# Masked products, updates and sampled updates of a linear attention, split into parts with a mixer product between the parts

## The chip, the cores and the metric

The kernel runs on one core of a Trainium2 chip. The metric is the device time of one launch in microseconds (us). Three runs of the kernel before gave 2438.61, 2433.31 and 2435.87 us; their median, 2435.87 us, is the time before. Engines are named as the profile names them: PE is TensorE with its matmuls, PEld its weight loads, DVE is VectorE, ACT is ScalarE, POOL is GpSimd, SP the engine that issues most loads.

## The reference

The reference is one step of a hybrid decoder of two layers (DEPTH = 2) over a prompt of 512 tokens and a sample group of 8 sequences with 4 new tokens each, 544 token rows in all. Each layer has two token mixers in parallel, a sparse attention (its output is A) and a gated linear attention, GLA (its output is B), and then a gated merge and a feed-forward part:

```python
def step(S, inp):
    qi, ki, vi, gi = inp
    b = jnp.cumsum(gi, axis=2)
    qe = qi * jnp.exp(b)
    att = jnp.where(tril, jnp.einsum('bhid,bhjd->bhij', qe, ki * jnp.exp(-b)), 0.0)
    o = jnp.einsum('bhij,bhjv->bhiv', att, vi) + jnp.einsum('bhid,bhdv->bhiv', qe, S)
    bl = b[:, :, -1:, :]
    S = jnp.exp(bl[:, :, 0, :, None]) * S + jnp.einsum('bhjd,bhjv->bhdv', ki * jnp.exp(bl - b), vi)
    return S, o
...
mix = jax.nn.sigmoid(g_ma) * (o_a @ w_pa) + jax.nn.sigmoid(g_mb) * (o_b @ w_pb)
x = x + mix @ w_out
```

GLA has 4 heads with keys of 64 and values of 128. The prompt's 512 tokens are 8 chunks of 64, in which the state S is carried from chunk to chunk; each of the 8 sampled sequences has one chunk of 4 tokens and a state of its own. The change touches `att` (the masked product), the last einsum of `step` (the update of the state) for the prompt and for the sampled sequences, and the order in which they stand to `o_a @ w_pa`. Everything is fp32.

## The kernel before

Every engine has a program of its own, written out by hand in the order in which it is to run; PE's begins at L788 and runs the two layers in a loop, and ACT and DVE have loops of the same shape. They are held together by semaphores alone. The activations stand transposed, features on the partitions and the 544 tokens in the free dimension, so that a product of a 128-column block of a weight is a chain of matmuls over the 128-row blocks of the contraction, each in two halves of 272 tokens (`product`, L809). In the trace each such matmul shows as two instructions with a weight load each.

PSUM has pools of slots that are taken in turn: T and S with two slots each, of two banks, and E. `claim` waits until the use of the slot before this one has been drained, that is until ACT or DVE has copied it out; `filled` is what the draining engine waits for. A product named X therefore cannot start on PE before the product two places ahead of it in the same pool has been drained. The names are tickets: `pa0` to `pa7` (the mixer products, T), `att0` to `att4` (the masked products, S), `up0` to `up7` (the updates of the prompt's state, T), `us0` to `us3` (the updates of the sampled states, T, two sequences each), `kd` and `kd4` (transposes of the decayed keys, S), `o8s`, `o8` (outputs of the sampled sequences, S), `o0` to `o3` (outputs of the four prompt tiles, S), and `on0` to `on3` (the sums of squares for the output norm, T).

The part in question comes once per layer, between the end of the sparse attention's softmax work and the merge:

- PE transposes the decayed keys (`kd`, L1264, and `kd4`, L1269), and ACT copies both out (L1708 to L1713).
- `first_mixer(m)` (L1275) is one of the eight 128-column blocks of `o_a @ w_pa`: four blocks of contraction, two halves, 16 matmuls in the trace with 128x272 outputs. It needs AT, whose last part DVE writes (`at_ready`). DVE's `gate_mixer(m)` (L2341) multiplies it out of PSUM with the merge gate, which ACT's sigmoid over `gaT` has to have made (`merge_gate`).
- The masked products (L1284 to L1294): for each of the four prompt tiles of 128 tokens, the 4 heads' products of 64x128 keys and 64x128 queries, and a small fifth for the sampled tokens. DVE multiplies each with a mask as it copies it out.
- The updates (L1298 to L1308): 8 chunks, 4 heads each, 64x64 weights. DVE adds each to the state carried on (`stt` at L2379, each needs the one before).
- `o8s` and `o8`: what the sampled queries read from their old states, and their outputs. Then the sampled updates (L1335 to L1343), which DVE adds to S0 after it has scaled S0 (L2391).
- `o0` to `o3` (L1345 to L1357): the prompt's outputs from masked products, values and states. ACT copies each out (L1726 to L1729).
- `out_norm(h)` (L1359): `mean_d` times the squares of head h. ACT squares all four heads after it has copied `o3` out (L1733, 1734), then takes the roots (`norm_root`, L424), and DVE turns each into the normed and gated output.

PE's order before is: `kd`, `kd4`, mixers 0 and 1, masked 0 to 4, mixer 2, updates 0 to 7, mixer 3, `o8s`, mixer 4, `o8`, sampled updates 0 to 3, mixer 5, `o0` to `o3`, mixer 6, `on0`, `on1`, mixer 7, and then the gate products `gb` and the products `pb` of the second mixer.

DVE's order before is: the last copies into AT, memsets and copies that spread the queries over `qz` and `qzs` (L2350 to L2361), `gate_mixer(0)`, the five masks, gates 1 and 2, the eight steps of the state, `kdb`, gates 3 and 4, the scaling of S0, the four sampled additions, gates 5 and 6, then the norms.

POOL writes the new states out after `gla_states` 1 and 2 and brings x back to its tile after `o3`; SP loads the mixer weights `pa0` and `pa1` into ring slots well ahead and refills each slot when its last product is filled.

Of the kernel before, what the change touches and what calls it, by code (L numbers as in the profile page):

```python
# [26 lines left out]
ALU = mybir.AluOpType  # L27
# [3 lines left out]
P = 128  # L31
D_MODEL, SEQ, DEPTH, NB, TS = 1024, 512, 2, 8, 4
PAST, PAGE = 2048, 128
HD, HEADS, G, R = 64, 8, 2, 4
STRIDE = 16
NS = NB * TS
# [11 lines left out]
GH, DK, DV, RANK = 4, 64, 128, 16  # L48
GL_HALF, GL_ROWS = 64, 104
CHUNK = 64  # L50
# [180 lines left out]
def build(nc, S, ins, outs):  # L231
# [3 lines left out]
    with ctx:  # L235
# [5 lines left out]
        PS = ctx.enter_context(nc.psum_tensor("PS", [P, 8, 512], F32))  # L241
# [22 lines left out]
        gmask_s = sb("gmask_s", NS)  # L264
# [77 lines left out]
        vT = xrows[:, 0:2560].rearrange("p (t n) -> p t n", n=512)  # L342
# [444 lines left out]
        def _(pe):  # L787
# [90 lines left out]
            for l in range(DEPTH):  # L878
# [396 lines left out]
                def first_mixer(m):  # L1275

                    w = ring[:, wload(f"pa{m // 4}"), :].rearrange("p (r n) -> p r n", n=512)
                    c0 = P * (m % 4)
                    product("T", f"pa{m}", lambda k: w[:, k, c0:c0 + P], lambda k: AT[:, k, :], R)

                pe.wait_ge(*S.at(pe, "at_ready", 1))
                first_mixer(0)
                first_mixer(1)
                for t in range(5):  # L1284

                    pe.wait_ge(*S.claim(pe, "S", f"att{t}"))
                    b = S.banks(pe, f"att{t}")
                    pe.nop().then_inc(*S.inc(pe, "settled"))
                    n = P if t < 4 else NS
                    for h in range(GH):  # L1290
                        hp, o = h // 2, HD * (h % 2)
                        mm = pe.matmul(PS[0:n, b + h % 2, n * hp:n * hp + n], kbT[o:o + HD, hp, P * t:P * t + n], qbT[o:o + HD, hp, P * t:P * t + n],
                                       start=True, stop=True)
                    mm.then_inc(*S.fill(pe, f"att{t}"))  # L1294
                first_mixer(2)


                for t in range(4):  # L1298
                    for c in range(2):
                        i = 2 * t + c  # L1300
                        pe.wait_ge(*S.claim(pe, "T", f"up{i}"))
                        b = S.banks(pe, f"up{i}")
                        pe.nop().then_inc(*S.inc(pe, "settled"))
                        for h in range(GH):
                            o = HD * (h % 2)
                            mm = pe.matmul(PS[o:o + HD, b, P * (h // 2):P * (h // 2) + P], kdm[CHUNK * c:CHUNK * c + CHUNK, t, HD * h:HD * h + HD],
                                           vT[CHUNK * c:CHUNK * c + CHUNK, t, P * h:P * h + P], start=True, stop=True)
                        mm.then_inc(*S.fill(pe, f"up{i}"))  # L1308
                first_mixer(3)
                pe.wait_ge(*S.at(pe, "qke_ready", 1))  # L1310
                pe.wait_ge(*S.at(pe, "s0_in"))
# [20 lines left out]
                        out = PS[:, b, 0:GH * NS].rearrange("p (a c f n) -> p a f c n", a=2, c=2, f=2)[:, a, hf]  # L1332
                        mm = pe.matmul(out.rearrange("p c (q t) -> p c q t", t=TS), o8s[:, hf, a, :], of_row, start=False, stop=(a == 1 and hf == 1))
                mm.then_inc(*S.fill(pe, "o8"))
                for q in range(4):  # L1335
                    pe.wait_ge(*S.claim(pe, "T", f"us{q}"))
                    b = S.banks(pe, f"us{q}")
                    for i in range(2):
                        for h in range(GH):
                            o = HD * (h % 2)  # L1340
                            mm = pe.matmul(PS[o:o + HD, b, 256 * i + P * (h // 2):256 * i + P * (h // 2) + P], kdb[0:NS, 2 * q + i, HD * h:HD * h + HD],
                                           vT[0:NS, 4, P * h:P * h + P], start=True, stop=True)
                    mm.then_inc(*S.fill(pe, f"us{q}"))  # L1343
                first_mixer(5)
                pe.wait_ge(*S.drained(pe, "att3"))  # L1345
                for t in range(4):
                    pe.wait_ge(*S.at(pe, "state", 1))
# [7 lines left out]
                            mm = pe.matmul(PS[:, b, P * h + CHUNK * c:P * h + CHUNK * c + CHUNK], states[:, i, h // 2, :],  # L1355
                                           qz[:, h, CHUNK * i:CHUNK * i + CHUNK], start=False, stop=(c == 1))
                    mm.then_inc(*S.fill(pe, f"o{t}"))  # L1357
                first_mixer(6)
                def out_norm(h):  # L1359

                    pe.wait_ge(*S.at(pe, "sq_o", h + 1))
# [435 lines left out]
        def _(dv):  # L1797
            S.phase(dv, "pro")

            def tt(out, a, b_, op):  # L1800
                return nc.vector.tensor_tensor(out, a, b_, op)  # L1801
# [16 lines left out]
            def bc(v, shape):  # L1818
                return v.broadcast_to(shape)
# [42 lines left out]
            for l in range(DEPTH):  # L1862
# [478 lines left out]
                def gate_mixer(m):  # L2341

                    dv.wait_ge(*S.filled(dv, f"pa{m}"))
                    b = S.banks(dv, f"pa{m}")
                    dv.wait_ge(*S.at(dv, "merge_gate", 1))
                    tt(two(gaT[:, m, :]), pair2(b), two(gaT[:, m, :]), ALU.mult).then_inc(*S.drain(dv, f"pa{m}"))
# [13 lines left out]
                    last = copy(qzs[:, :, :, TS * c:TS * c + TS],  # L2360
                                qz[:, c:GH:2, SEQ:NT].rearrange("p a (b t) -> p b a t", t=TS))  # L2361
                last.then_inc(*S.inc(dv, "qke_ready"))
                gate_mixer(0)
                for t in range(4):
                    dv.wait_ge(*S.filled(dv, f"att{t}"))
                    b = S.banks(dv, f"att{t}")
                    tt(attT[:, t].rearrange("p (a o) n -> p o a n", o=2), PS[:, b:b + 2, 0:256].rearrange("p o (a n) -> p o a n", a=2),
                       bc(gmask[:, :].unsqueeze(1).unsqueeze(1), [P, 2, 2, P]), ALU.mult).then_inc(*S.drain(dv, f"att{t}"))
                dv.wait_ge(*S.filled(dv, "att4"))
                b = S.banks(dv, "att4")  # L2370
                tt(att_s[0:NS].rearrange("p (a o) n -> p o a n", o=2), PS[0:NS, b:b + 2, 0:2 * NS].rearrange("p o (a n) -> p o a n", a=2),
                   bc(gmask_s[0:NS, :].unsqueeze(1).unsqueeze(1), [NS, 2, 2, NS]), ALU.mult).then_inc(*S.drain(dv, "att4"))
                gate_mixer(1)
                gate_mixer(2)
                for i in range(8):
                    dv.wait_ge(*S.filled(dv, f"up{i}"))
                    b = S.banks(dv, f"up{i}")
                    for c in range(2):
                        last = stt(states[:, i + 1, c, :], states[:, i, c, :], eb[:, c, CHUNK * i + CHUNK - 1:CHUNK * i + CHUNK],  # L2379
                                   PS[:, b, P * c:P * c + P], ALU.mult, ALU.add)  # L2380
                    last.then_inc(*S.drain(dv, f"up{i}"))
                    dv.wait_ge(*S.drained(dv, f"up{i}"))
                dv.nop().then_inc(*S.inc(dv, "gla_states"))
                dv.wait_ge(*S.drained(dv, "kd4"))
                tt(kdb[0:NS, :, :], bc(kdm[0:NS, 4, :].unsqueeze(1), [NS, NB, 256]), bc(batch_hot[0:NS, :].unsqueeze(2), [NS, NB, 256]), ALU.mult).then_inc(*S.inc(dv, "kdb"))
# [5 lines left out]
                    last = tt(S0[:, :, a, :], S0[:, :, a, :], bc(ebS[:, :, a:a + 1], [P, NB, DV]), ALU.mult)  # L2391
                last.then_inc(*S.inc(dv, "dve_step"))
                dv.wait_ge(*S.last(dv, "dve_step"))
                for q in range(4):
                    dv.wait_ge(*S.filled(dv, f"us{q}"))
                    b = S.banks(dv, f"us{q}")
                    v = S0[:, 2 * q:2 * q + 2, :, :].rearrange("p b a v -> p (b a v)")
                    tt(v, PS[:, b, :], v, ALU.add).then_inc(*S.drain(dv, f"us{q}"))
                dv.wait_ge(*S.drained(dv, "us2"))
                dv.wait_ge(*S.drained(dv, "us3"))  # L2400
                dv.nop().then_inc(*S.inc(dv, "gla_states"))
                gate_mixer(5)
                gate_mixer(6)
                for h in range(GH):
                    if h == 1:
# [108 lines left out]
```

## Time and profile before

| | |
|---|---|
| median of three runs | 2435.87 us (2433.31 to 2438.61) |
| the profiled execution | 2436.56 us, its span 2434.8 us |
| PE busy | 2385.6 us, 98% of the span |
| DVE, ACT busy | 809.5 us (33%), 539.0 us (22%) |
| mean granted TensorE clock | 0.986 |
| the stretch from `kd4` to the end of mixer 7, first layer | 515.0 to 580.8 us of the span |
| the same in the second layer | 1719.4 to 1785.2 us |

How to read it: the span is the time from the first to the last instruction of one profiled execution, and positions such as 515.0 are microseconds from its start. Busy shares say how full an engine is; the granted clock is the share of full speed that TensorE was given, 1.00 for 2.4 GHz and 0.50 for 1.2 GHz. In the answers below each line of the timeline has a start, a length, the engine, the line of the kernel, the operation, what it writes and reads, its shape and how many instructions were merged into it; in square brackets stands the idle time before them and what ended it.

### The profile page before, as it was taken

What the parts mean: (1) busy time and instruction counts of PE and PEld (TensorE: products, weight loads), DVE (VectorE), ACT (ScalarE), POOL (GpSimd) and SP (SyncE); (2) the same over time, 40 slices, a digit from 0 to 9 for tenths busy, and PEclk for the clock granted to TensorE, in tenths of its full rate; (3) what the DMA queues carried; (4) which work ended last, traced back from release to release, by engine and by line L of the source; (5) the groups of instructions that cost most, each with busy time, mean ns of one, the idle gap of its engine ahead of it and who ended that gap; (6) DMA issues with size and microseconds to landing.
All of it is one profiled execution on the core that took longest, in us unless ns stands there. A gap on an engine that the chain in (4) does not pass through costs nothing.

```text
span 2434.8 us, 30974 instructions
## 1 busy us (share of the span) xinstructions
PE 2385.6 (98%) x13063; PEld 1926.0 (79%) x13063; DVE 809.5 (33%) x1893; ACT 539.0 (22%) x1085; POOL 104.8 (4%) x190
## 2 busy tenths in 40 slices
PE   8999899999999999999999999999999999999999
PEld 7787766678888888888888877667788888888887
DVE  4554545544114222210035544465441232222000
ACT  2353124432011111110013522244220111111000
POOL 4010010001000000000000100000000000000000
PEclk9999999999999999999999999999899999999999
DMA  7553421112222222212373544111122222222222
GB/s 231 186 200 142 197 95 52 32 41 89 70 72 70 70 78 79 66 51 72 77 265 130 219 162 183 53 36 36 49 95 72 69 70 70 70 82 65 63 72 73
DMA packets 186988, 237.55 MB, mean 98 GB/s; under 512 B 38047, under 2 KB 172704, under 8 KB 181984
## 3 DMA queue, kind: packets, MB, share of 16 engines
q1 hardware_dynamic: 175208, 133.11, 18.4%
q0 software_dynamic: 11200, 102.36, 11.1%
q8 instruction: 104, 1.70, 0.3%
q14 instruction: 32, 0.26, 0.0%
q10 hardware_dynamic: 444, 0.12, 0.0%
HBM read 222.76 MB, written 21.11 MB: 100 GB/s over the span
## 4 chain that ended last, share of the span: by engine, by line
PE 93%; DVE 4%; DMA 1%; ACT 1%; issue 1%; SPq 0%; POOL 0%; DVEq 0%; ACTq 0%; POOLq 0%
PE PS L818 52%; PE PS L1441 13%; PE PS L840 6%; PE PS L938 4%; PE PS L866 2%; DVE arena L1810 2%; PE PS L926 2%; PE PS L437 2%; PE PS L1219 2%; PE PS L1208 2%; PE PS L1136 1%; DMA arena<-in_cache_kv_slc_dram,idx 1%; ACT arena L1472 1%; PE PS L1181 1%; PE PS L1147 1%
## 5 line engine op out<-in xcount | busy, mean ns | idle before, releaser
L818 PE MATMUL PS<-hT,ring 128*128 128x272 f32 x4352 | 1010.1, 394 | 2.5 <-DVE small L2254 1.9
L818 PEld LDWEIGHTS PS<-hT,ring 128*128 128x128 f32 x4352 | 827.9, 191 | 175.5 <-issue 8.7
L1472 ACT ACTIVATE arena<-PS 64x512 f32<-64x512 f32 (+13 forms) x467 | 231.3, 518 | 1185.8 <-PE PS L818 559.8
L1441 PE MATMUL PS<-arena,ring 128*128 128x272 f32 x1408 | 323.7, 393 | 0.0
L1441 PEld LDWEIGHTS PS<-arena,ring 128*128 128x128 f32 x1408 | 268.0, 191 | 54.1
L1810 DVE COPY arena<-PS 64x512 f32<-64x512 f32 (+4 forms) x201 | 142.7, 710 | 268.6 <-PE PS L818 98.4
L1801 DVE TENSOR_TENSOR arena<-PS,arena 128x544 f32<-128x544 f32 (+3 forms) x124 | 76.0, 624 | 398.2 <-PE PS L818 380.9
L818 PE MATMUL PS<-arena,ring 128*128 128x272 f32 x768 | 177.2, 393 | 3.1 <-DVE arena L1801 3.1
L818 PEld LDWEIGHTS PS<-arena,ring 128*128 128x128 f32 x768 | 146.2, 191 | 33.5 <-DVE arena L1801 4.0
L1807 DVE SCALAR_TENSOR_TENSOR arena<-arena,prm 128x32 f32<-128x32 f32 (+1 forms) x176 | 88.1, 500 | 249.1 <-ACT arena L1472 245.8
L1801 DVE TENSOR_TENSOR xT<-PS,xT 128x544 f32<-128x544 f32 x32 | 23.2, 724 | 386.3 <-PE PS L1441 303.2
L840 PE MATMUL PS<-ring,hT 128*128 128x256 f32 x640 | 146.3, 390 | 0.6 <-ACT qT L1472 0.6
L840 PEld LDWEIGHTS PS<-ring,hT 128*128 128x128 f32 x640 | 124.1, 196 | 21.8 <-issue 3.3
L938 PE MATMUL PS<-arena 128*128 128x256 f32 (+1 forms) x576 | 136.5, 382 | 2.3 <-DVE arena L1810 0.5
L938 PEld LDWEIGHTS PS<-arena 128*128 128x128 f32 x576 | 103.2, 198 | 19.5 <-DVE arena L1810 5.2
L1472 ACT ACTIVATE arena<-arena 128x544 f32<-128x544 f32 (+5 forms) x102 | 68.1, 694 | 73.1 <-DVE arena L1807 71.5
L1472 ACT ACTIVATE arena<-xT,prm 128x544 f32<-128x544 f32 x32 | 23.5, 745 | 266.4 <-DVE xT L1801 264.7
L1472 ACT ACTIVATE arena<-arena,small 128x128 f32<-128x128 f32 (+3 forms) x128 | 70.4, 556 | 40.4 <-DVE small L1807 39.9
L926 PE MATMUL PS<-ident,arena 128*128 128x128 f32 (+1 forms) x576 | 73.0, 270 | 0.0
L818 PE MATMUL PS<-qT,ring 128*128 128x272 f32 x256 | 70.2, 435 | 0.0
L926 PEld LDWEIGHTS PS<-ident,arena 128*128 128x128 f32 (+1 forms) x576 | 63.6, 142 | 7.6 <-issue 1.5
L818 PEld LDWEIGHTS PS<-qT,ring 128*128 128x128 f32 x256 | 53.2, 213 | 13.9 <-issue 2.1
(309 smaller groups left out, 1665.3 us busy)
## 6 DMA issues: line engine op xcount, KB each, us to landing
ring<-in_w_up_dram SPq DMA_DIRECT2D x88, 512.0 KB, 4.6
ring<-in_w_in_dram SPq DMA_DIRECT2D x68, 512.0 KB, 4.8
ring<-in_w_down_dram SPq DMA_DIRECT2D x32, 384.0 KB, 3.8
ring<-in_w_down_dram SPq DMA_DIRECT2D x32, 320.0 KB, 4.5
arena<-in_state_kv_win_dram POOLq DMA_DIRECT2D x4, 2048.0 KB, 20.4
ring<-in_w_out_dram SPq DMA_DIRECT2D x16, 512.0 KB, 4.1
out_dram<-in_state_kv_win_dram POOLq DMA_DIRECT2D x2, 4064.0 KB, 23.8
ring<-in_w_in_dram SPq DMA_DIRECT2D x16, 256.0 KB, 5.0
```

Source lines behind the costliest of these rows:

```text
L437: mm = pe.matmul(PS[HD * g:HD * g + HD, VBANKS[qt % 2], P * r:P * r + P], kv[:, t, 1 + br, P + HD * g:P + HD * g + HD], PTp[j % 2][:, g, P ...
L818: mm = pe.matmul(PS[0:m, b + a, 0:HALF], weight(k), rhs(k)[:, HALF * a:HALF * a + HALF], start=(k == 0), stop=(k == nk - 1))
L840: mm = pe.matmul(out, hT[:, k, P * t:P * t + nt], w[:, k, c0:c0 + n], start=(k == 0), stop=(k == KC - 1))
L866: mm = pe.matmul(PS[:, b + a, 0:HALF], w[:, k, P * i:P * i + P], raw[:, k, HALF * a:HALF * a + HALF], start=(k == 0), stop=(k == KC - 1))
L926: mm = pe.transpose(PS[:, b + r // 4, P * (r % 4):P * (r % 4) + n], XB[s][0:n, 8 * q + r, P * c:P * c + P], ident[0:n, 0:n])
L938: mm = pe.matmul(out, w1[:, c, 4 * q + pr, :, :], XT[j % 2][:, pr, :, 0:n], start=(q == 0 and pr == 0), stop=(q == 1 and pr == 3))
L1208: mm = pe.matmul(PS[:, b + g, 0:P * (qt + 1)], qT[HD * g:HD * g + HD, r, P * qt:P * qt + P], kT[HD * g:HD * g + HD, br, 0:P * (qt + 1)], s ...
L1441: mm = pe.matmul(PS[:, b + a, 0:HALF], w[:, k, :], aT[:, 11 * half + k, HALF * a:HALF * a + HALF], start=(half == 0 and k == 0), stop=(hal ...
L1472: return nc.scalar.activation(out, in_, func, **kw)
L1801: return nc.vector.tensor_tensor(out, a, b_, op)
L1807: return nc.vector.scalar_tensor_tensor(out=out, in0=a, scalar=s_, in1=b_, op0=op0, op1=op1)
L1810: return nc.vector.tensor_copy(out, a)
```

## The change

Nothing is computed differently. On PE the masked and the update products become helpers, and the order is: masked 0 to 2, mixer 0, masked 3 and 4, mixer 1, updates 0 to 3, mixer 2, updates 4 to 7, mixer 3, `o8s`, mixer 4, `o8`, sampled updates 0 and 1, mixer 5, sampled updates 2 and 3, mixer 6, `o0` to `o3`, `on0`, `on1`, mixer 7. On DVE the masks, the steps of the state and the additions move in the same manner against the gates: three masks come ahead of gate 0. ACT, POOL and SP are as before. (The diff is cut to its moved calls; the bodies of the helpers are those shown above.)

```diff
 # PE
-                pe.wait_ge(*S.at(pe, "at_ready", 1))
-                first_mixer(0)
-                first_mixer(1)
-                for t in range(5):
+                def masked(t):
...
+                def update(i):
...
+                for t in range(3):
+                    masked(t)
+                pe.wait_ge(*S.at(pe, "at_ready", 1))
+                first_mixer(0)
+                for t in range(3, 5):
+                    masked(t)
+                first_mixer(1)
+                for i in range(4):
+                    update(i)
                 first_mixer(2)
-                for t in range(4):
-                    for c in range(2):
-                        i = 2 * t + c
...
+                for i in range(4, 8):
+                    update(i)
                 first_mixer(3)
...
-                for q in range(4):
+                def sampled_update(q):
...
+                sampled_update(0)
+                sampled_update(1)
                 first_mixer(5)
+                sampled_update(2)
+                sampled_update(3)
+                first_mixer(6)
                 pe.wait_ge(*S.drained(pe, "att3"))
                 for t in range(4):
...
                     mm.then_inc(*S.fill(pe, f"o{t}"))
-                first_mixer(6)
 # DVE
-                gate_mixer(0)
-                for t in range(4):
+                def masked(t):
...
-                gate_mixer(1)
-                gate_mixer(2)
-                for i in range(8):
+                def update(i):
...
+                for t in range(3):
+                    masked(t)
+                gate_mixer(0)
+                masked(3)
+                dv.wait_ge(*S.filled(dv, "att4"))
...
+                gate_mixer(1)
+                for i in range(4):
+                    update(i)
+                gate_mixer(2)
+                for i in range(4, 8):
+                    update(i)
...
-                for q in range(4):
+                def sampled_update(q):
...
+                sampled_update(0)
+                sampled_update(1)
+                gate_mixer(5)
+                sampled_update(2)
+                sampled_update(3)
                 dv.wait_ge(*S.drained(dv, "us2"))
                 dv.wait_ge(*S.drained(dv, "us3"))
                 dv.nop().then_inc(*S.inc(dv, "gla_states"))
-                gate_mixer(5)
                 gate_mixer(6)
```

## Rows read from the trace of the kernel before

**Rows 1.** The page, part 1 (busy time) and part 4 (chain that ended last, by engine)

```profile
PE 2385.6 (98%) x13063; PEld 1926.0 (79%) x13063; DVE 809.5 (33%) x1893; ACT 539.0 (22%) x1085; POOL 104.8 (4%) x190
...
PE 93%; DVE 4%; DMA 1%; ACT 1%; issue 1%; SPq 0%; POOL 0%; DVEq 0%; ACTq 0%; POOLq 0%
```

**Rows 2.** Table by stretch, first layer; after the busy times: clock, DMA share, GB/s

```profile
515.00:530.00 15.00, 14.28 (x93) 11.46 (x94) 8.67 (x19) 8.91 (x6) 0.00 (x0) 1.00 0.11 37
530.00:536.40 6.40, 5.32 (x65) 3.64 (x62) 4.79 (x15) 0.00 (x0) 0.00 (x0) 0.89 0.01 3
536.40:543.00 6.60, 6.60 (x22) 4.85 (x24) 2.88 (x3) 0.00 (x0) 0.74 (x1) 0.59 0.08 22
...
549.80:555.10 5.30, 5.30 (x65) 4.74 (x65) 3.15 (x4) 0.28 (x1) 0.00 (x0) 0.71 0.01 3
555.10:560.80 5.70, 5.70 (x19) 4.47 (x18) 0.69 (x1) 0.00 (x0) 4.22 (x6) 0.67 0.32 98
```

**Rows 3.** Timeline, first layer, from `kd4` to DVE's first gate

```profile
514.19 1.30 ACT L1472 ACTIVATE arena<-PS 128x1024 f32<-128x1024 f32 x2 [9.89 <-PE PS L1264]
...
515.01 7.57 PE L818 MATMUL PS<-qT,ring 128*128 128x272 f32 x32
...
519.64 0.30 DVE L1810 COPY arena<-arena 128x64 f32<-128x64 f32 x2
...
520.74 0.72 DVE L1801 TENSOR_TENSOR arena<-PS,arena 128x544 f32<-128x544 f32 x1 [0.81 <-ACT arena L1472]
```

**Rows 4.** Timeline, first layer, masked products, mixer 2, updates, start of mixer 3

```profile
522.51 1.16 PE L1292 MATMUL PS<-qbT,kbT 64*128 64x128 f32 x16
523.27 1.29 DVE L1801 TENSOR_TENSOR kv_kT<-PS,gmask 128x512 f32<-128x512 f32 x2 [1.80 <-PE PS L1292]
...
524.11 1.31 PE L1292 MATMUL PS<-qbT,kbT 64*128 64x128 f32 x16 [0.44 <-DVE kv_kT L1801]
...
525.95 3.94 PE L818 MATMUL PS<-qT,ring 128*128 128x272 f32 x16
...
529.81 0.66 PE L1306 MATMUL PS<-xT,arena 64*64 64x128 f32 x8
...
532.30 1.29 PE L1306 MATMUL PS<-xT,arena 64*64 64x128 f32 x16 [0.34 <-DVE kv_kT L1807]
...
536.37 6.59 PE L818 MATMUL PS<-qT,ring 128*128 128x272 f32 x16
```

**Rows 5.** Timeline, first layer, from `o8`'s first matmul to mixer 5

```profile
547.77 1.07 PE L1327 MATMUL PS<-arena,xT 32*128 32x32 f32 x8
...
549.78 1.72 PEld L1341 LDWEIGHTS PS<-xT,arena 32*64 32x64 f32 x32
...
550.99 1.50 DVE L1801 TENSOR_TENSOR arena<-PS,arena 128x512 f32<-128x512 f32 x2
...
555.10 5.78 PE L818 MATMUL PS<-qT,ring 128*128 128x272 f32 x16
```

**Rows 6.** Timeline, first layer, from the end of `o3` to mixer 7

```profile
571.38 3.89 PE L818 MATMUL PS<-qT,ring 128*128 128x272 f32 x16
...
572.25 2.30 ACT L1472 ACTIVATE arena<-arena 128x544 f32<-128x544 f32 x4
574.57 1.28 ACT L1472 ACT_TABLE_LOAD   x1
...
575.10 2.23 PE L818 MATMUL PS<-arena,mean_d 128*128 128x272 f32 x8
...
576.22 0.71 ACT L1472 ACTIVATE kbT<-PS,cols 128x544 f32<-128x544 f32 x1 [0.37 <-PE PS L818]
...
577.16 3.83 PE L818 MATMUL PS<-qT,ring 128*128 128x272 f32 x16
```

**Rows 7.** Timeline, second layer: mixer 3, sampled updates, mixer 5

```profile
1740.65 5.22 PE L818 MATMUL PS<-qT,ring 128*128 128x272 f32 x16
...
1752.68 6.33 PE L1341 MATMUL PS<-xT,arena 32*64 32x128 f32 x64
...
1758.94 6.30 PE L818 MATMUL PS<-qT,ring 128*128 128x272 f32 x16
```

More of the change, by code:

```diff
@@ L1294, in _ @@
                     mm.then_inc(*S.fill(pe, f"att{t}"))
-                first_mixer(2)
-                for t in range(4):
-                    for c in range(2):
-                        i = 2 * t + c
[L1301 to L1308, printed above, removed]
+                def update(i):
+                    t, c = i // 2, i % 2
+                    pe.wait_ge(*S.claim(pe, "T", f"up{i}"))
+                    b = S.banks(pe, f"up{i}")
+                    pe.nop().then_inc(*S.inc(pe, "settled"))
+                    for h in range(GH):
+                        o = HD * (h % 2)
+                        mm = pe.matmul(PS[o:o + HD, b, P * (h // 2):P * (h // 2) + P], kdm[CHUNK * c:CHUNK * c + CHUNK, t, HD * h:HD * h + HD],
+                                       vT[CHUNK * c:CHUNK * c + CHUNK, t, P * h:P * h + P], start=True, stop=True)
+                    mm.then_inc(*S.fill(pe, f"up{i}"))
+                for t in range(3):
[7 more added lines that the diff above has]
+                    update(i)
+                first_mixer(2)
+                for i in range(4, 8):
+                    update(i)
                 first_mixer(3)
@@ L2368, in _ @@
                        bc(gmask[:, :].unsqueeze(1).unsqueeze(1), [P, 2, 2, P]), ALU.mult).then_inc(*S.drain(dv, f"att{t}"))
[L2369 to L2372, printed above, removed]
-                gate_mixer(1)
-                gate_mixer(2)
-                for i in range(8):
+                def update(i):
                     dv.wait_ge(*S.filled(dv, f"up{i}"))
@@ L2382, in _ @@
                     dv.wait_ge(*S.drained(dv, f"up{i}"))
+                for t in range(3):
[3 more added lines that the diff above has]
+                dv.wait_ge(*S.filled(dv, "att4"))
+                b = S.banks(dv, "att4")
+                tt(att_s[0:NS].rearrange("p (a o) n -> p o a n", o=2), PS[0:NS, b:b + 2, 0:2 * NS].rearrange("p o (a n) -> p o a n", a=2),
+                   bc(gmask_s[0:NS, :].unsqueeze(1).unsqueeze(1), [NS, 2, 2, NS]), ALU.mult).then_inc(*S.drain(dv, "att4"))
+                gate_mixer(1)
[4 more added lines that the diff above has]
+                    update(i)
                 dv.nop().then_inc(*S.inc(dv, "gla_states"))
```

## The prediction

> **What bounds the kernel now.** I read the page first: PE is busy for 98% of the span and carries 93% of the chain that ended last [rows 1]. So a change of order is worth what it does to PE's own line: its idle time, and its clock. Then the table by stretch for the part that the change touches, for the clock [rows 2], and then the timeline of the same part, for who waits for whom [rows 3 to 6]. The second layer repeats the first 1204.4 us later (mixer 0 at 1719.4 for 515.0) and differs only in where the clock falls [rows 7].
>
> In the table the clock is at full speed from 515.0 to 530.0, masked products included, and falls in two places [rows 2]. A mean of 0.89 over the 6.4 us of the updates is 1.4 us at half speed, so the clock fell near 535.0, some 5 us into them; then 5.4 us of the stretch with mixer 3 are at half speed (0.59 of 6.6 us). A mean of 0.71 in the sampled updates is 3.1 us at half speed, and 3.8 us more follow under mixer 5. What PE did before each fall was small products: the updates of 64x64 weights at the pace of DVE's additions, and `o8` and the sampled updates with 32 rows [rows 4, 5]. What it costs: mixer 3 takes 6.59 us where mixer 2 takes 3.94 (+2.65), mixer 5 takes 5.78 (+1.84), and the sampled updates last 5.32 us (549.78 to 555.10), where 32 of their 64 loads took 1.72 us at full speed, so some 3.6 in all (+1.7) [rows 4, 5]. That is 6.2 us. In the second layer it is 5.22 - 3.94 = 1.28, 6.30 - 3.94 = 2.36 and 6.26 - 3.6 = 2.7 [rows 7], 6.3 us. **12.5 us, 0.5% of the time, is all that the clock can give back here.**
>
> **The masked products, moved ahead of mixer 0.** Now mixers 0 and 1 run from 515.01 for 7.5 us, and under them DVE fills `qz`, until 519.94, and ACT makes the sigmoid that gate 0 waits for [rows 3]. The masked products come at 522.51, when DVE is nearly free. In the new order `att0` and `att1` can go as soon as ACT has drained `kd` and `kd4` (515.5), and are done by about 516.3. `att2` needs the slot of `att0`, which DVE drains, and DVE's first mask is still queued behind the `qz` copies: it starts at 519.95, takes 0.65 (half of 1.29), and from such a drain to PE's next start it is 0.15 (the first of the two masks from 523.27 ends at 523.95, `att2` starts at 524.11) [rows 4]. So `att2` starts at 520.75 and mixer 0, behind it, at 521.3. Queued behind that wait are `att2`, mixer 0 and all the rest of PE's line; mixer 0 itself would have needed nothing. Masked 3 and 4 later cost 0.7, half of the 1.16 of a pair and a small one of 0.2, with no wait left. Together 6.3 + 0.7 = 7.0 us, where the five took 3.44 (522.51 to 525.95): **+3.55 us** per layer. PE idles for 4.4 of these.
>
> **The updates in two groups.** Eight take 6.56 us (529.81 to 536.37) at DVE's pace. The first of a group finds its slot free; from the first's start to the fourth's it is 2.49 (532.30), plus 0.6 for the fourth itself (0.66 for eight instructions): 3.1 us for a group, 6.2 for two [rows 4]: **-0.35 us**. Gates 1 and 2 stand at the head of each group on DVE, as both do before the first now.
>
> **The sampled updates in two groups.** Mixer 5 takes the slot of `us0`, whose addition ends at 551.7, since DVE scales S0 until then [rows 5]; it can start 2.0 us after 549.78. Behind mixer 5, `us3` needs mixer 5's slot, which gate 5 (0.72) drains about 1.0 us after `us2` begins, so that group takes 2.0 too. 4.0 against 3.6 at full speed: **+0.4 us**.
>
> **Mixer 6, taken from behind `o3`.** It now runs from 571.38, while ACT copies `o3` out, squares four heads (until 574.55), loads the table for the roots (until 575.85) and takes the first root; `on0` and `on1` follow at 575.10, mixer 7 at 577.16 [rows 6]. So behind `o3` there are 577.16 - 571.38 = 5.78 us, 3.72 of them mixer 6. Without it `on0` waits for the first square (about 572.9), `on1` follows, and mixer 7 needs the slot of `on0`, which the root drains: 575.85 + 0.71 + 0.15 = 576.7. That is 5.35 us in place of 2.06: **+3.3 us**, with PE idle for 3.5 of them. ACT's work is what was hidden, and its cover is gone.
>
> At nothing I cost: DVE's gates and POOL's stores, which come a few us later but aren't waited for before the merge, 30 us on; SP's queue, where the load behind `pa0`'s slot waits for mixer 3 and that behind `pa1`'s for mixer 7, and each is wanted only after the gate products; and the reading of the squares on DVE, whose normed heads are wanted 30 us later.
>
> With the clock at full speed throughout, a layer is thus 3.55 - 0.35 + 0.4 + 3.3 = **6.9 us longer**, against 6.25 that the clock costs now.
>
> **What the clock costs after the change.** No row shows PE idle for 4.4 us in this part. From below it is nothing, if the clock stayed. I take it that it falls, since it fell under the updates, where PE still worked for 5.32 of 6.40 us [rows 2], and this stretch is emptier. What a fall costs the products behind it is in four rows: 1.28, 1.84, 2.36, 2.65 us, mean 2.0 [rows 4, 5, 7]. So mixer 0 and its neighbours lose 2.0. The stretch from `o8` to `us1` is 4.0 us of small products where now 7.3 stand (547.77 to 555.10); the clock fell 4.3 us into it (552.0), so an even chance of a loss of 2.6 (2.0, and some of the sampled updates themselves): 1.3. Each group of updates is 3.1 us where the clock fell after 5: one in four, 2.0 each, 1.0 for the two. Sum 4.3. **Per layer 6.9 - 6.25 + 4.3 = +4.95, for two +9.9 us.** The profiled execution took 2436.56, so 2446.5; it stands 0.7 above the median of the runs, so **2445.8 us**.
>
> The row shows the clock falling under a busy PE whose products are small. The Trainium skill ("TensorE: Matmul & The Clock Gate", section "HAM oscillation — how this bites in real kernels") says that bursts of matmuls with waits between them lose the clock again and again, and asks for denser work. Its advice speaks for the split of the updates and against the wait ahead of mixer 0; taken for the splits alone it is the first rival below.
>
> **Rivals.**
>
> *Faster: the clock decides.* If the splits hold the clock at full speed and the two waits turn out hidden, a layer gains 6.25 + 0.35 - 0.4 = 6.2: 2423.5 us. For it: each group of small products is shorter than what PE had done of them before the clock fell. It decides from the point where the two waits together cost less than 6.2 us of the 6.85 that I give them, with no new fall. Against it: the mask is behind 5 us of copies on DVE, ACT's chain behind `o3` is fixed, and PE has nothing to run in between. 0.08.
>
> *No difference.* The waits are as I say, but the clock stays up in the short idle stretch or costs the least seen, 1.28, and never falls elsewhere: +0.65 to +1.95 per layer, 2437 to 2440 us. 0.14.
>
> *Slower still: the splits don't do what they say.* The clock falls in every group of updates and of sampled updates, because a group of small products between two mixers is enough. Then all of 2.0 + 2.6 + 2 x 2.0 = 8.6 is paid: 6.9 - 6.25 + 8.6 = 9.25 per layer, 2454 us. The row for it is that the updates leave PE waiting between any two of them [rows 4]. The same page of the Trainium skill, in "A second HAM failure mode: psum-queue depth-cycling", describes a clock that oscillates with short idle times between groups of matmuls; that is this rival's mechanism. 0.20.
>
> **How the numbers follow.** My forecast has 0.58. A difference of 0.2%, 4.9 us, is about what a measurement of this kernel can tell from none, its runs being 5.3 us apart. Slower by more are the forecast and the last rival: 0.78. The same is 0.14, faster 0.08. The forecast's own range is from one fall per layer (6.9 - 6.25 + 2.0 = 2.65, 2441.2) to one where the sampled updates and one group of updates lose theirs too (2.0 + 2.6 + 2.0 = 6.6, so +7.25, 2450.4). With the bounds of the rivals on either side, 2438 to 2454 us.
>
> **What would show it.** In the timeline after: PE idle for 4 us or more before the third masked product, ended by DVE; mixer 0 longer than 5 us; two idle stretches behind `o3`, of about 1.5 and 2 us, ended by ACT; updates in groups of about 3.1 us. In the table by stretch: a clock below 1.00 ahead of mixer 0, and near 1.00 in mixers 2, 3 and 4. I am wrong if `att2` starts within a microsecond of `att1`, if mixer 7 starts less than 4 us behind `o3`, or if the clock stays at 1.00 behind the idle stretch.

## The result, and the profile after

The changed kernel takes 2453.43 us in the median of four runs (2451.59 to 2454.04), the kernel before 2437.01 beside it; the ratio is 1.0067, with a 95% interval of 1.0055 to 1.0079. It is slower by 16.4 us. A second set of six runs, on another occasion, gave 2449.64 us (2444.31 to 2453.32) and a ratio of 1.0054 (1.0041 to 1.0068); both belong to the result, and why the sets differ is told below.

The page after: part 1, then part 4 by engine.

```profile
span 2449.8 us, 30970 instructions
...
PE 2386.7 (97%) x13063; PEld 1920.0 (78%) x13063; DVE 809.7 (33%) x1893; ACT 539.2 (22%) x1085; POOL 105.1 (4%) x190
...
PE 92%; DVE 4%; ACT 1%; DMA 1%; issue 1%; SPq 0%; DVEq 0%; ACTq 0%; POOLq 0%
```

PE has the same 13063 matmuls and is busy for 1.1 us more than in [rows 1], in a span that is 15.0 us longer. What was lost is idle time, and a clock that fell at other places. PE's waits, longest first (total, times, longest); the three of this part are:

```profile
PE PS L1289 <- DVE kv_kT L1815: 8.1, 2, 4.1
PE PS L818 <- ACT kbT L1486: 3.3, 2, 1.7
...
PE PS L818 <- ACT arena L1486: 2.8, 2, 1.4
```

L1289 is the masked product, which waited for DVE for 0.44 us at most before [rows 4]. L818 behind ACT is `on0` and mixer 7, which did not wait for it. Now the timeline of the first layer, which answers to [rows 3, 4]:

```profile
513.63 1.31 ACT L1486 ACTIVATE arena<-PS 128x1024 f32<-128x1024 f32 x2 [9.89 <-PE PS L1264]
...
514.91 1.16 PE L1289 MATMUL PS<-qbT,kbT 64*128 64x128 f32 x16 [0.38 <-ACT arena L1486]
...
519.09 0.30 DVE L1824 COPY arena<-arena 128x64 f32<-128x64 f32 x2
519.30 1.28 DVE L1815 TENSOR_TENSOR kv_kT<-PS,gmask 128x512 f32<-128x512 f32 x2
...
520.13 1.23 PE L1289 MATMUL PS<-qbT,kbT 64*128 64x128 f32 x8 [4.06 <-DVE kv_kT L1815]
...
521.28 5.43 PE L818 MATMUL PS<-qT,ring 128*128 128x272 f32 x16
...
526.64 0.96 PE L1289 MATMUL PS<-qbT,kbT 64*128 64x128 f32 x16
...
527.53 3.93 PE L818 MATMUL PS<-qT,ring 128*128 128x272 f32 x16
...
531.39 0.65 PE L1301 MATMUL PS<-xT,arena 64*64 64x128 f32 x8
...
534.53 5.59 PE L818 MATMUL PS<-qT,ring 128*128 128x272 f32 x16
...
540.05 0.65 PE L1301 MATMUL PS<-xT,arena 64*64 64x128 f32 x8
...
543.24 3.90 PE L818 MATMUL PS<-qT,ring 128*128 128x272 f32 x16
```

The first two masked products are done by 516.1. The third stands until DVE has copied `qz` out to the end and masked the first: 4.06 us. From its start to mixer 0's it is 1.15 us for eight instructions, and mixer 0 takes 5.43, where a mixer at full speed takes 3.93. A group of four updates is 3.1 us long (531.39 to 534.53). The mixer behind the first group takes 5.59 us, the one behind the second 3.90. The sampled part and the tail, same view, which answer to [rows 5, 6]:

```profile
553.96 2.66 PE L1350 MATMUL PS<-xT,arena 32*64 32x128 f32 x32
...
556.55 6.56 PE L818 MATMUL PS<-qT,ring 128*128 128x272 f32 x16
...
563.04 1.98 PE L1350 MATMUL PS<-xT,arena 32*64 32x128 f32 x32
...
565.01 3.91 PE L818 MATMUL PS<-qT,ring 128*128 128x272 f32 x16
...
581.00 2.10 PE L818 MATMUL PS<-arena,mean_d 128*128 128x272 f32 x8 [1.42 <-ACT arena L1486]
...
582.61 1.28 ACT L1486 ACT_TABLE_LOAD   x1
...
584.76 3.90 PE L818 MATMUL PS<-qT,ring 128*128 128x272 f32 x16 [1.66 <-ACT kbT L1486]
```

Mixer 5 takes 6.56 us. `on0` waits for ACT's first square; mixer 7 waits until the table is loaded (583.89) and the root taken. The table by stretch for the same part (columns as in [rows 2]):

```profile
516.10:520.10 4.00, 0.00 (x0) 0.00 (x1) 3.70 (x10) 3.97 (x3) 0.00 (x0) 0.68 0.00 0
520.10:526.60 6.50, 6.47 (x24) 4.94 (x24) 1.17 (x2) 3.29 (x2) 0.00 (x0) 0.67 0.01 3
...
531.40:534.50 3.10, 2.43 (x33) 1.73 (x33) 2.45 (x7) 0.00 (x0) 0.00 (x0) 1.00 0.00 0
534.50:540.00 5.50, 5.50 (x18) 4.10 (x16) 0.61 (x2) 0.00 (x0) 0.00 (x0) 0.69 0.00 0
...
556.50:563.00 6.50, 6.50 (x18) 4.74 (x16) 0.69 (x1) 0.00 (x0) 0.00 (x0) 0.59 0.01 3
...
579.40:584.70 5.30, 2.28 (x10) 1.48 (x9) 0.05 (x1) 4.97 (x8) 1.12 (x2) 1.00 0.62 198
```

The clock fell in the idle stretch ahead of the third masked product, behind the first group of updates and in the first sampled group. It stayed at full speed behind `o3`, where PE was busy for 2.28 of 5.3 us.

One number sums this up. From the first transpose of `kd` to the first gate product it was 67.8 us in either layer before (513.06 to 580.83 and 1717.44 to 1785.19). After, it is 76.0 and 76.1 (512.50 to 588.50 in the first). That is 16.6 us for both layers, as much as the medians differ (16.4). I call this the stretch below. The two profiled spans differ by 15.0 us: the changed kernel's was 0.6 us shorter ahead of the first stretch and 1.0 between the two, where the change moves nothing.

### The profile page after: what moved, and what is told of

The parts are those of the page before. It is cut to its first block, busy times and chain, and to the rows that moved or that the text cites. A ratio compares the mean times of both kernels' runs of the same rounds, so it can differ in the third digit from the quotient of the medians.

```text
span 2449.8 us, 30970 instructions
## 1 busy us (share of the span) xinstructions
PE 2386.7 (97%) x13063; PEld 1920.0 (78%) x13063; DVE 809.7 (33%) x1893; ACT 539.2 (22%) x1085; POOL 105.1 (4%) x190
## 4 chain that ended last, share of the span: by engine, by line
PE 92%; DVE 4%; ACT 1%; DMA 1%; issue 1%; SPq 0%; DVEq 0%; ACTq 0%; POOLq 0%
PE PS L818 51%; PE PS L1455 13%; PE PS L840 6%; PE PS L938 4%; PE PS L866 2%; DVE arena L1824 2%; PE PS L926 2%; PE PS L437 2%; PE PS L1219 2%; PE PS L1208 2%; PE PS L1136 1%; DMA arena<-in_cache_kv_slc_dram,idx 1%; ACT arena L1486 1%; PE PS L1181 1%; PE PS L1147 1%
## 5 line engine op out<-in xcount | busy, mean ns | idle before, releaser
L818 PE MATMUL PS<-hT,ring 128*128 128x272 f32 x4352 | 1010.0, 394 | 2.5 <-DVE small L2268 1.9
L818 PEld LDWEIGHTS PS<-hT,ring 128*128 128x128 f32 x4352 | 825.6, 190 | 177.8 <-issue 8.7
L1815 DVE TENSOR_TENSOR arena<-PS,arena 128x544 f32<-128x544 f32 (+3 forms) x124 | 76.1, 625 | 387.7 <-PE PS L818 367.4
L818 PE MATMUL PS<-arena,ring 128*128 128x272 f32 x768 | 177.2, 393 | 3.2 <-DVE arena L1815 3.2
L818 PEld LDWEIGHTS PS<-arena,ring 128*128 128x128 f32 x768 | 145.8, 190 | 33.9 <-DVE arena L1815 4.0
L1486 ACT ACTIVATE arena<-arena 128x544 f32<-128x544 f32 (+5 forms) x102 | 68.1, 694 | 72.7 <-DVE arena L1821 71.2
L1486 ACT ACTIVATE arena<-arena,small 128x128 f32<-128x128 f32 (+3 forms) x128 | 70.4, 556 | 40.4 <-DVE small L1821 40.0
L818 PE MATMUL PS<-qT,ring 128*128 128x272 f32 x256 | 74.4, 452 | 3.3 <-ACT kbT L1486 3.3
L926 PE MATMUL PS<-ident,arena 128*128 128x128 f32 (+1 forms) x576 | 72.7, 269 | 0.0
L818 PEld LDWEIGHTS PS<-qT,ring 128*128 128x128 f32 x256 | 55.3, 222 | 19.4 <-issue 6.8
L926 PEld LDWEIGHTS PS<-ident,arena 128*128 128x128 f32 (+1 forms) x576 | 63.2, 141 | 7.7 <-issue 1.5
```

The lines of the kernel that those rows point to most:

```text
L818: mm = pe.matmul(PS[0:m, b + a, 0:HALF], weight(k), rhs(k)[:, HALF * a:HALF * a + HALF], start=(k == 0), stop=(k == nk - 1))
L926: mm = pe.transpose(PS[:, b + r // 4, P * (r % 4):P * (r % 4) + n], XB[s][0:n, 8 * q + r, P * c:P * c + P], ident[0:n, 0:n])
L1486: return nc.scalar.activation(out, in_, func, **kw)
```

## The experiments

Nine further kernels ran, and the changed kernel again. Times are medians; the ratio is to the kernel before, run beside each (2436.96 to 2437.99 us), and is not simply the quotient of the two medians.

| kernel | us | ratio to before, interval | stretch, layers 1 and 2 |
|---|---|---|---|
| changed (first, again) | 2453.4, 2449.6 | 1.0067, 1.0054 | 76.0, 76.1; again 75.1, 72.5 |
| masks ahead of qz copies | 2435.7 | 0.9995 (0.9985 to 1.0004) | 70.4, 67.1 |
| mixer 6 back behind o3 | 2445.1 | 1.0024 (1.0012 to 1.0037) | 72.6, 72.7 |
| both | 2429.4 | 0.9965 (0.9951 to 0.9979) | 67.1, 63.7 |
| before, updates split alone | 2431.4 | 0.9984 (0.9974 to 0.9994) | 64.7, 66.4 |
| both, updates inside mixers | 2425.0 | 0.9941 (0.9923 to 0.9958) | 63.2, 63.2 |
| the same, sampled ones too | 2424.5 | 0.9945 (0.9928 to 0.9961) | 62.2, 62.2 |
| before, tail alone | 2443.1 | 1.0026 (1.0016 to 1.0036) | 71.1, 71.1 |
| before, front alone | 2448.1 | 1.0039 (1.0025 to 1.0053) | 75.2, 74.8 |
| before, all inside mixers | 2424.3 | 0.9949 (0.9936 to 0.9961) | 62.0, 62.0 |

**The front undone, without moving PE's work.** In the changed kernel DVE's masks 0 to 2 go ahead of what PE never waited for:

```diff
                 nc.vector.memset(states[:, 0, :, :], 0.0).then_inc(*S.inc(dv, "state"))
+                def masked(t):
...
+                for t in range(3):
+                    masked(t)
                 for h in range(GH):
...
-                for t in range(3):
-                    masked(t)
                 gate_mixer(0)
```

> The changed kernel with one thing moved on DVE: its first three masks stand ahead of the copies that fill qz. My theory, that the third masked product waits for DVE's first mask and that the idle time drops the clock: PE's idle 4.1 us ahead of it goes, the table shows a clock of 1.00 up to mixer 0, mixer 0 takes 3.9 us in place of 5.43. Some 6.3 us per layer, 12.6 us faster than the changed kernel, about 2441 us. Rival, that the wait only moves (the qz copies come later on DVE and hold gate 0 and the updates): within 3 us of 2453. Second rival, that the clock falls there for the small masked products alone and not for the idle time: the idle time goes (8.4 us for both layers, 2445) but mixer 0 still takes over 5 us.

PE's timeline there, first layer, and the table by stretch:

```profile
518.73 1.16 PE L1289 MATMUL PS<-qbT,kbT 64*128 64x128 f32 x16 [0.38 <-ACT arena L1486]
520.32 0.72 PE L1289 MATMUL PS<-qbT,kbT 64*128 64x128 f32 x8 [0.43 <-DVE kv_kT L1815]
520.96 3.94 PE L818 MATMUL PS<-qT,ring 128*128 128x272 f32 x16
```

```profile
518.00:521.00 3.00, 2.19 (x27) 1.65 (x27) 1.46 (x3) 2.97 (x4) 0.00 (x0) 1.00 0.67 229
521.00:525.00 4.00, 4.00 (x19) 3.09 (x20) 3.54 (x7) 3.98 (x2) 0.00 (x0) 1.00 0.01 4
```

The wait is 0.43 us, the clock stays at 1.00, mixer 0 takes 3.94. The masked products are the same and in the same place on PE, so the second rival falls: it was the idle time. The first rival falls too, since nothing behind it waits for the later copies. Mixer 0 starts 4.6 us after the first transpose of `kd` in place of 8.8. The gain looks larger than forecast: 17.8 us against the first set of the changed kernel, 14.0 against the second; the stretches give 14.6. But part of it is the clock elsewhere. The first layer, where the clock fell in the same places as in the changed kernel, is 5.6 us shorter; the second is 9.0 shorter, and 1.7 of that is a fall behind the updates that didn't come, 1.6 a smaller loss in the sampled part. Like with like, the front is worth 5.6 us per layer, less than the 6.3 forecast.

**The tail undone.** PE's `first_mixer(6)` moved back behind the loop over `o0` to `o3`.

> The changed kernel with mixer 6 put back behind o3. My theory: the 5.35 us between the end of o3 and mixer 7 take mixer 6 in again, so 3.3 us per layer, 6.6 us faster than the changed kernel, about 2447 us, with PE not waiting for ACT behind o3. Rival, that those waits cost nothing because mixer 6 merely does its work earlier: 2453, with o0 starting 3.8 us earlier and everything behind the norms unchanged.

The waits on ACT left the list; the stretch is 3.4 us shorter in each layer, as forecast (3.3). The medians give 8.3 us against the first set and 4.5 against the second, on both sides of the 6.6 that was expected. The rival, that nothing is gained, falls by the stretches: the clock fell in the same places in both traces.

**Both undone, the splits kept.**

> The changed kernel with both edits, the masks ahead of the qz copies and mixer 6 behind o3; the split of the updates and of the sampled updates stays. If the two losses are separate they add: 12.6 + 6.6 = 19.2 us faster than the changed kernel, about 2434 us, which would be 3 us faster than the kernel before. If the clock is what they share, less than the sum: 2437 to 2440.

2429.4 us, 5 us faster than expected and faster than before. The two losses are separate: by the stretches they save 14.6 and 6.8, together 21.3 (152.1 to 130.8), which is their sum within 0.1. This trace has its falls where the one with the early masks has them, so the clock doesn't blur the sum.

**The updates' split alone, in the kernel before.** `first_mixer(3)` and its gate stand between `up3` and `up4`.

> The kernel before with the updates alone split into two groups of four, mixer 3 between them (so o8s follows the second group directly). By my reckoning of the prediction, where a group of four loses the clock one time in four, a layer gains 0.35 + 2.0 - 0.5 = 1.85: 3.7 us faster than before, about 2433 us. Rival, that a group of four drops the clock as often as the eight did: only the 0.35 per layer, about 2436 us, and mixer 3 or mixer 4 at over 5 us in the trace.

2431.4 us, a ratio of 0.9984 (0.9974 to 0.9994): faster, by 3.9 us as the ratio has it and by 6.0 as the medians have it, where I reckoned 3.7. The rival's gain of 0.35 us per layer, 0.7 in all, lies outside the interval. The trace has both outcomes, mixer 3 between the groups in the first layer and then in the second:

```profile
532.88 3.90 PE L818 MATMUL PS<-qT,ring 128*128 128x272 f32 x16
```

```profile
1732.72 5.59 PE L818 MATMUL PS<-qT,ring 128*128 128x272 f32 x16
```

The same group of four, the same mixer, and the clock falls in one layer and not in the other. A group of 3.1 us sometimes loses it and sometimes not. In the six traces with groups of four (24 groups, the repeated changed kernel among them) it fell behind 8, in seven of them behind the first group of its layer.

**The updates one by one inside the mixers.** `product` got a call after each block of contraction, and the updates take slots of pool S, so that a mixer can stay open in pool T:

```diff
                 first_mixer(1)
-                for i in range(4):
-                    update(i)
-                first_mixer(2)
-                for i in range(4, 8):
-                    update(i)
-                first_mixer(3)
+                first_mixer(2, lambda k: update(k))
+                first_mixer(3, lambda k: update(4 + k))
...
-                    pe.wait_ge(*S.claim(pe, "T", f"up{i}"))
+                    pe.wait_ge(*S.claim(pe, "S", f"up{i}"))
```

> The kernel with masks ahead of the qz copies and mixer 6 behind o3, and the updates one by one inside mixers 2 and 3, one behind each of their four blocks of contraction; the updates take their PSUM slots from the other pool for that. If the updates cost what they do because PE waits for DVE between them and the clock falls under them, a layer loses 2 x 3.1 us of groups and gets 8 x 0.45 = 3.6 back, and the clock's loss behind the updates (1.7 in the changed kernel's trace) goes: 4.3 us per layer, 8.6 us faster than the kernel with both edits and groups of four, about 2426 us if that one is at 2434. Rival, that small products cost their own time on PE wherever they stand and the clock falls for their share of the work alone: under 2 us.

> As the kernel with the updates inside mixers 2 and 3, with the sampled updates also one by one inside mixer 5. In the changed kernel's trace the sampled updates lose 0.7 us and mixer 5 2.65 us to the clock. If the clock stays up: 3.3 us and a wait of 0.3 per layer, 7 us faster than the kernel with only the updates inside. If the 2 us of o8 in front of them are enough to drop it: no gain, and mixer 5 slow from its start.

2425.0 and 2424.5 us. The first is 4.3 us faster than the kernel with both edits, half of the 8.6 that I expected, and more than the rival said (under 2). The intervals of the two ratios overlap a little; the stretches also differ by 4.3 (130.8 to 126.4). In the second layer, where neither trace has a fall behind the updates, they differ by only 0.5. The second kernel shortens the stretch by 2.1 us for both layers in place of 7, and the time by nothing that the medians can tell. Its clock is at 1.00 in the whole part, where mixer 5 of the first one took 5.59 us; but a block and a sampled update take 2.13 us there, so that four such updates cost 4.6 us in place of the 4.0 of two groups. Why the updates cost more than I had taken is seen in the last kernel.

**The parts alone, the changed kernel again, and the best order on the old front.** The first takes only mixer 6 ahead of `o0`, the second only the new places of the masked products, both in the kernel before.

> The kernel before with one thing of the change alone: mixer 6 ahead of o0 in place of behind o3. The wait behind o3 costs 3.3 us per layer by my reckoning: 6.6 us slower than before, about 2444 us. Putting it back in the changed kernel gave 8.3 us between medians from different sets of runs; if there is more to it than the wait (a second place that the moved mixer slows), this run shows 4 us per layer too. If mixer 6 in its new place also keeps the clock up between the sampled updates and o0, less: 2441.

> The kernel before with the front of the change alone: masked 0 to 2 ahead of mixer 0, masked 3 and 4 ahead of mixer 1, on PE and DVE, with the updates and the sampled updates unsplit. By the trace of the changed kernel: the wait and what stands around it 3.55 us, mixer 0 1.5 and the third masked product 0.65 to the clock, 5.7 us per layer: 11.4 us slower than before, about 2449 us. Rival, that the masks' place behind the qz copies costs nothing once the updates stand as before: 2437.

> The changed kernel again, beside the others of this call: 1.0067 of the kernel before as in its first runs, about 2453 us. The two parts alone should then add up to it with what the two splits give or take: 11.4 + 6.6 = 18.0 against 16.4, so the splits together are worth 1.6 us at most.

> The kernel before with its own front and tail, and only the updates one by one inside mixers 2 and 3 and the sampled updates one by one inside mixer 5, each behind one of the four blocks of contraction. If the early masked products give nothing of themselves, this is as fast as the kernel with all inside, 2424 to 2425 us, with the clock at 1.00 in the whole part. If they do, 2 us or more slower than that one.

The tail alone costs 6.1 us (2443.1 against 2437.0), 3.4 and 3.3 in the stretches, so there is no second cost in it. Its waits are the two behind `o3`, of 1.42 and 1.66 us:

```profile
576.81 2.10 PE L818 MATMUL PS<-arena,mean_d 128*128 128x272 f32 x8 [1.42 <-ACT arena L1472]
580.57 3.90 PE L818 MATMUL PS<-qT,ring 128*128 128x272 f32 x16 [1.66 <-ACT kbT L1472]
```

The front alone costs 11.1 us by the medians (2448.1), 9.5 by the ratio, against 11.4 expected; its six runs lie wide apart (2441.1 to 2453.1), and the rival's 2437 is out. It has the one wait for DVE and the clock that falls in it (the trace is that of its slowest run, with 14.4 us in the stretches):

```profile
PE PS L1289 <- DVE kv_kT L1813: 8.1, 2, 4.1
```

```profile
518.50:522.30 3.80, 0.00 (x0) 0.00 (x0) 3.50 (x10) 3.78 (x1) 0.00 (x0) 0.83 0.00 0
522.30:530.40 8.10, 8.07 (x41) 6.11 (x41) 1.98 (x4) 3.30 (x2) 0.00 (x0) 0.66 0.00 0
```

By ratios the parts alone add to 1.0065, the whole, run beside them, is 1.0054 (1.0041 to 1.0068). So the splits together would give 2.7 us back, which is within the intervals.

The changed kernel again: its trace has the clock falling behind the second group of updates in the first layer, behind neither in the second, and mixer 5 losing less. These are the four mixers 0 to 3 of its first layer:

```profile
522.93 6.15 PE L818 MATMUL PS<-qT,ring 128*128 128x272 f32 x16
529.90 3.93 PE L818 MATMUL PS<-qT,ring 128*128 128x272 f32 x16
536.90 3.90 PE L818 MATMUL PS<-qT,ring 128*128 128x272 f32 x16
543.92 5.59 PE L818 MATMUL PS<-qT,ring 128*128 128x272 f32 x16
```

The same program on the same data gave 2444.98 us in this execution and 2451.59 in the first profiled one. Their stretches differ by 4.5 us through the clock alone. Another 3.8 us lie between the two stretches, where the change touches nothing: from 1440 to 1490 us the granted clock is 0.93 in the first execution and 1.00 in this one. Ahead of the first stretch this one is 1.7 us longer. The six runs lie in two bunches: three at 2444.3 to 2446.6 us with a mean granted clock of 0.988, three at 2452.7 to 2453.3 with 0.985, and the four runs of the first set are of the second kind (0.985 and 0.986). A clock lower by 0.003 over 2450 us is some 7 us of full speed, an estimate that fits the 8 us between the bunches. That is why the two sets differ.

The last kernel, with the front of before, is as fast as the one with the early masked products: 2424.3 against 2424.5 us. So masking early gives nothing of itself. It beats both kernels of this case, before by 12.7 us. Its timeline in the first layer, a block, an update, a block, and the table by stretch:

```profile
525.87 1.18 PE L818 MATMUL PS<-qT,ring 128*128 128x272 f32 x4
...
526.98 0.41 PEld L1304 LDWEIGHTS PS<-xT,arena 64*64 64x64 f32 x8 [0.36 <-issue]
526.98 0.65 PE L1304 MATMUL PS<-xT,arena 64*64 64x128 f32 x8
527.56 0.76 PEld L818 LDWEIGHTS PS<-qT,ring 128*128 128x128 f32 x4 [0.17 <-issue]
527.57 1.19 PE L818 MATMUL PS<-qT,ring 128*128 128x272 f32 x4
...
528.68 0.65 PE L1304 MATMUL PS<-xT,arena 64*64 64x128 f32 x8
```

```profile
526.00:540.00 14.00, 14.00 (x116) 9.13 (x120) 6.21 (x20) 0.00 (x0) 0.00 (x0) 1.00 0.01 2
540.00:546.00 6.00, 6.00 (x50) 4.85 (x43) 4.72 (x5) 0.60 (x1) 0.74 (x1) 1.00 0.61 196
546.00:555.00 9.00, 9.00 (x86) 6.57 (x86) 3.63 (x6) 0.28 (x1) 0.00 (x0) 1.00 0.01 2
555.00:575.00 20.00, 20.00 (x137) 18.05 (x137) 5.77 (x5) 7.39 (x11) 6.88 (x10) 1.00 0.48 165
```

The clock is at 1.00 throughout and PE does not wait for DVE's additions any more. But a block and an update take 1.70 us (526.98 to 528.68), where a block in an unbroken mixer is a quarter of 3.86, 0.97: an update costs 0.73 us here too, not the 0.45 that I had taken. It is nearly as long as the 0.76 at DVE's pace. The weight loads show where the time is: of each 1.70 us they are busy for 0.76 + 0.41 and idle for 0.36 + 0.17, at either switch, with nothing in the profile that they wait for. What the kernel gains is the clock, and little of the waits; that is why the updates inside the mixers gave half of what I expected.

## Why the prediction was right

It said slower, 2445.8 us, between 2438 and 2454, and it is 2453.4 in the first set and 2449.6 in the second. The mechanisms were those named: a wait for DVE in front, a wait for ACT in the tail, and a clock that falls in the first. Against the first set the sum fell short by 7.6 us. That 2453.4 lies inside is in part luck: the forecast's own range ended at 2450.4, and the upper bound of 2454 was taken from the slower rival. One of the signs named did not come: mixer 2 was to run near 1.00 and ran at 0.69.

- **The wait of the third masked product.** Forecast: start 5.74 us behind the point where mixer 0 stood. Measured: 520.13 against 514.45, 5.68. PE idle 4.1 (4.4 forecast). Shown by its removal through DVE's order alone and by the front on its own.
- **The tail.** Forecast 3.3 us per layer; the stretch with mixer 6 put back is 3.4 shorter, the tail alone 3.4 and 3.3 longer. The clock did not fall behind `o3` in the first trace. In three other traces (the tail alone, the repeated one, the early masks) it fell there in one layer each, and cost nothing, since PE waits for ACT then and mixer 7 starts 3.8 us after `on0` all the same.
- **The groups of updates.** 3.1 us each, as forecast.
- **The sampled groups.** The second took 1.98 us (2.0 forecast), with mixer 6 straight behind it.
- **What the clock costs after the change** is the step that was mis-sized: 4.3 us per layer in the sum. Measured in the first trace: 2.0 in front (0.5 in the third masked product, which took 1.15 us to mixer 0's start where the early masks give 0.64, and 1.5 in mixer 0; 2.0 forecast), 1.7 behind the first group of updates (1.0 forecast), and 3.3 in the sampled part (0.68 in the updates and 2.65 in mixer 5, 1.3 forecast). That is 7.0, 2.7 more per layer, 5.4 for both, most of the 7.6; 2.0 of the 2.7 are the sampled part. Another 1.1 is the kernel before, whose median came to 2437.01 for the 2435.87 from which I had counted. The even chance for the stretch from `o8` to `us1` was wrong: the clock fell there in both layers of all six traces that keep the group of two. For a group of updates, one in four was put too low by the 8 of 24.
- **The rest**, 0.6 us per layer, is in small terms: the masked products 3 and 4 took 0.9 us in place of 0.7, the third 0.1 more at full speed than forecast, the two groups of updates 6.3 in place of 6.2. What is left, some 0.2, stays open.

The rival of a clock that falls in every small group had 0.20, with 2454 us. It was nearer in its number than my forecast, but not in its mechanism: one of two groups of updates per layer kept the clock in the first trace, and three of four in the repeated one. The faster rival had its price right in kind: with both waits gone the same splits are 8.1 us faster than before (2429.4 against 2437.5), not the 12.4 that it claimed, since the splits as made don't hold the clock everywhere.

The rule of the Trainium skill ("TensorE: Matmul & The Clock Gate", section "HAM oscillation — how this bites in real kernels"), that bursts with waits between them lose the clock, agrees with these traces on the wait of 4.06 us. By it alone the small products, packed without a wait, would be safe. The sampled updates run back to back behind `o8` (PE busy for all of 5.30 us in [rows 2]) and they or the mixer behind them lose the clock in both layers of all ten traces that keep two or four of them together, so the measurement goes further than the sentence.

## What to carry to other kernels

Before filler work is put between small pieces, ask what it covered where it stood: a mixer product was cover for DVE's 5 us of copies at the front and for ACT's squares and table load at the tail, and without it 4.1 us of PE's idle time appeared in front and 3.1 in the tail, in each layer. Where a product waits for a slot, look at what is queued ahead of the drain on the draining engine; moving DVE's three masks ahead of unurgent copies took that wait away with PE's order left as it was, 5.6 us per layer. Small updates kept the clock when they were spread one by one between the blocks of a full product: no fall behind them in the six layers of the three kernels that did so, where groups of four were followed by one in 8 of 24. For that the two need PSUM slots of different pools. And compare like with like: with two bunches 8 us apart, the places where the clock fell have to be the same in two traces before their difference is read as an edit's.

## What the runs showed of the hardware

- A wait of some 4.05 us ahead of the third masked product dropped the clock in all eight layers of the four traces that have it (mixer 0 took 5.14 to 6.15 us). With a wait of 0.43 us and the same products, mixer 0 took 3.93 or 3.94 in all eight layers of four other traces.
- The same group of four updates, 3.1 us of 64x64 products between two full mixers, was followed by a mixer at 3.90 us in one layer and at 5.59 in the other of the same execution. So one trace doesn't price such an edit: the changed kernel has runs near 2445 and near 2453 us.
- The clock fell under back-to-back matmuls too: in `o8` and the sampled updates, most of them with 32 rows, PE shows no idle time, and mixer 5 behind them took 5.78 to 6.61 us in the traces of before and of the first run after.
- With PE at work for only 2.28 of 5.30 us behind `o3`, in full-size products, the clock stayed at 1.00 there; in three other traces with this tail it fell in one of the two layers.
- Switching between a mixer's blocks and updates costs PE time without a wait for another engine: a pair takes 1.70 us, where a block in an unbroken mixer takes 0.97 and a second update directly behind a first some 0.5 (two take 1.17, one 0.65), so some 0.2 us a pair.
